# The delta-rule inverse built for all heads at once on 32x32 diagonal blocks, with the scan and the first head norms placed among the gated units

## The reference, cut to what matters

```python
kk = where(strict, k @ k.T * ratio, 0)        # ratio = exp(gc_i - gc_j), causal
a_mat = eye + beta[:, None] * kk
u_v = triangular_solve(a_mat, beta * v)       # unit lower triangular
w_k = triangular_solve(a_mat, beta * gamma * k)
# scan over the chunks, state s:
u = u_v - w_k @ s
o = (q * gamma) @ s + (q @ k.T * ratio) @ u
s = decay * s + (k * exp(gc_last - gc)).T @ u
```

## Time and profile before

| | |
|---|---|
| median of 3 runs | 2479.71 us |
| span of the profiled execution, which is its own time from first to last instruction | 2478.5 us |
| busy in it: TensorE, VectorE, ScalarE, GpSimd | 97%, 70%, 28%, 6% |
| `mixers`, from the first transpose (208.6 us) to the first product of `mix_out` (399.1 us) | 190.5 us |

### The profile page before, as it was taken

The page is one execution under the profiler, slowest core; times in us unless marked ns, Lnnn a source line. Parts: engine busy times, 40 slices in busy tenths (PEclk is TensorE's granted clock), DMA queues, the critical chain, the costliest instruction groups (busy, mean ns, idle before and its releaser), DMA issues. The chain is left out here.

```text
span 2478.5 us, 34266 instructions
## 1 busy us (share of the span) xinstructions
PE 2395.5 (97%) x13948; PEld 1947.8 (79%) x13948; DVE 1727.4 (70%) x2710; ACT 687.3 (28%) x1264; POOL 141.0 (6%) x127
## 2 busy tenths in 40 slices
PE   8998889999999999999999899999999999999997
PEld 6886878987788888887765588888888888888886
DVE  6665777846788874749788787666666886666653
ACT  2212443012211110423677613222202112222200
POOL 0001001001000012000121010000010001000001
PEclk9999989999999999999999999999999999999999
DMA  5220002421233264322200072333463552232341
GB/s 186 76 77 1 3 19 94 147 84 60 85 95 101 92 210 143 127 77 78 76 18 1 35 268 72 100 96 95 163 237 101 186 190 66 94 102 94 127 141 64
DMA packets 70332, 252.81 MB, mean 102 GB/s; under 512 B 7808, under 2 KB 8096, under 8 KB 69664
## 3 DMA queue, kind: packets, MB, share of 16 engines
q1 hardware_dynamic: 69888, 250.08, 30.5%
q10 hardware_dynamic: 288, 0.54, 0.1%
HBM read 248.50 MB, written 2.10 MB: 101 GB/s over the span
## 5 line engine op out<-in xcount | busy, mean ns | idle before, releaser
L393 PE MATMUL psum<-rounded_n,rounded_high 128*128 128x512 f32 x1856 | 736.2, 397 | 4.4 <-DVE rounded_n_low L547 1.8
L395 PE MATMUL psum<-rounded_n,rounded_ring 128*128 128x512 f32 x1856 | 723.9, 390 | 0.0
L394 PE MATMUL psum<-rounded_n_low,rounded_high 128*128 128x512 f32 x1856 | 723.8, 390 | 0.0
L347 DVE TENSOR_TENSOR rounded_ring<-ring,rounded_high 128x1024 fp32r<-128x1024 f32 (+1 forms) x360 | 445.8, 1239 | 38.7 <-ACT rounded_high L330 26.7
L393 PEld LDWEIGHTS psum<-rounded_n,rounded_high 128*128 128x128 f32 x1856 | 349.4, 188 | 85.2 <-issue 7.3
L394 PEld LDWEIGHTS psum<-rounded_n_low,rounded_high 128*128 128x128 f32 x1856 | 349.4, 188 | 76.5 <-issue 5.5
L395 PEld LDWEIGHTS psum<-rounded_n,rounded_ring 128*128 128x128 f32 x1856 | 349.2, 188 | 73.3
L345 DVE CAST rounded_high<-ring 128x1024 fp32r<-128x1024 f32 (+1 forms) x347 | 248.5, 716 | 190.1 <-PE psum L395 183.0
L393 PE MATMUL psum<-rounded_arena,rounded_high 128*128 128x512 f32 x720 | 281.2, 391 | 4.4 <-DVE rounded_ring L347 4.4
L394 PE MATMUL psum<-rounded_arena,rounded_high 128*128 128x512 f32 x720 | 281.0, 390 | 0.0
L395 PE MATMUL psum<-rounded_arena,rounded_ring 128*128 128x512 f32 x720 | 281.0, 390 | 0.0
(11 more groups left out here) (479 smaller groups left out, 2899.4 us busy)
## 6 DMA issues: line engine op xcount, KB each, us to landing
ring<-in_w_up SPq DMA_DIRECT2D x132, 512.0 KB, 3.4
ring<-in_w_down SPq DMA_DIRECT2D x48, 512.0 KB, 3.5
n_low<-in_mod_w SPq DMA_DIRECT2D x48, 512.0 KB, 5.2
arena<-in_mod_w SPq DMA_DIRECT2D x48, 512.0 KB, 5.2
ring<-in_w_ab_in SPq DMA_DIRECT2D x37, 512.0 KB, 3.5
ring<-in_w_mix_in SPq DMA_DIRECT2D x31, 512.0 KB, 3.4
ring<-in_w_sc_in SPq DMA_DIRECT2D x24, 512.0 KB, 5.3
ring<-in_w_down SPq DMA_DIRECT2D x24, 384.0 KB, 3.1
```

What stands on the lines that cost most here:

```text
L347: nc.vector.tensor_tensor(self.rounded(raw), raw, self.rounded(high), ALU.subtract).then_inc(self.weights_split, 1)
L393: self.nc.tensor.matmul(out, w_high, x_high, start=first, stop=False)
L394: self.nc.tensor.matmul(out, w_high, x_low, start=False, stop=False)
L395: return self.nc.tensor.matmul(out, w_low, x_high, start=False, stop=last)
```

## The change

It touches the projection in a few places and rewrites the order of `mixers`.

- **Projection.** `masks` and its DMA go. `mask` multiplies `ratio` by beta as well (4 instructions of 128x128 per head for one of 128x512), `key_tail` multiplies `tail` by beta, and ScalarE copies the 32x32 diagonal blocks of `ratio` into `ratio_c` (`ratio_blocks`, 4 copies). `beta_scale` and the beta in `scan_solved` go. The tiles CK and CQ change places.
- **The inverse.** For levels 1 to 16 only the 16 diagonal 32x32 blocks of each head matter; those of all 4 heads and chunks fit one 128x512 tile. `key_pieces` makes them directly, `first_inverse` does level 0, and four levels follow for all heads at once: 64 products of 32x32x32, a mask, 64 products, a subtraction, and a 32x32-block transpose on VectorE. Two joins give the 64x64 and the 128x128 blocks: two rounds of products each, with copies by ScalarE, and six placing copies on GpSimd. So 24 steps become 4, with the retention between them.
- **The units.** `decayed_pair` makes the halves of queries and keys that a level uses in one 128x512 instruction with an interleaved access pattern, for two. The units 1 and 2 alternate between two pairs of banks (`room`), and their small uses wait for the `take` before the last.
- **The order.** The scan begins at the fifth use, and the first head norms, gates and weight splits stand among units 1 and 2. The filler products of the scan go; 12 stay at the end. The inverse's results are kept in other buffers.

The diff, cut to its core:

```diff
@@ mixer_projection
-            sp.dma_start(k.masks[:], k.dram["masks"]).then_inc(late_landed, 16)
+            def ratio_blocks():
+                act.wait_ge(masked, HEADS)
+                for i in range(4):
+                    rows = slice(32 * i, 32 * i + 32)
+                    nc.scalar.copy(k.ratio_c[rows, :]..., k.ratio[rows, :, :]...[:, :, :, rows])
@@ mask
-                nc.vector.tensor_tensor(r, r, tri, ALU.mult).then_inc(masked, 1)
+                for c in range(TT):
+                    i, r = c * HEADS + h, k.ratio[:, h, c * P:(c + 1) * P]
+                    last = nc.vector.scalar_tensor_tensor(r, r, k.beta[:, i:i + 1], k.const("upto"),
+                                                          ALU.mult, ALU.mult)
@@ mixers, TensorE
+        def piecewise(out, keys, values):
+            for h in range(HEADS):
+                for c in range(TT):
+                    for i in range(4):
+                        last = nc.tensor.matmul(out[rows32(i), piece(h, c)], keys[rows32(i), piece(h, c)],
+                                                values[rows32(i), piece(h, c)], start=True, stop=True)
+        def inverse_times(n):
+            pe.wait_ge(inverse, n)
+            piecewise(k.psum[:, D0, :], k.an, k.xt).then_inc(crossed, 1)
+        def inverse_update(n):
+            pe.wait_ge(mixed_up, n)
+            piecewise(k.psum[:, D0 + 1, :], k.xn, k.pt).then_inc(copied, 1)
-        for x in range(D_STEPS):
-            if x + 1 < D_STEPS:
-                below(HEADS + x + 1)
-            update(HEADS + x)
-            use(x)
+        key_pieces()
+        key_halves()
+        turn(0)
+        inverse_times(1)
+        query_products(0)
+        inverse_update(1)
+        turn(1)
+        query_products(1)
+        inverse_times(2)
...
+        ret_values(7)
+        join_second()
+        use(0)
+        join_third()
+        use(1)
+        join_fourth()
+        use(2)
+        use(3)
+        scan_solve(0)
+        use(4)
+        scan_out(0)
+        use(5)
+        scan_keys(1)
...
+        scan_out(3)
+        use(13)
+        use(14)
+        for i in range(4):
+            norm_sums(pe, i)
+        use(15)
+        use(16)
+        for i in range(3):
+            norm_spread(pe, i)
...
+        pe.wait_ge(valued, 4)
+        for _ in range(8):
+            nc.tensor.matmul(k.psum[:, D0 + 1, 3 * P:T], k.const("ident"), k.const("ones"), start=True, stop=True)
+        for i in (6, 7):
+            norm_sums(pe, i)
@@ mixers, VectorE
+        def first_inverse():
+            dve.wait_ge(paired, 1)
+            link(nc.vector.tensor_tensor(fours(k.ntc, P), pairs_of(D0, 0, P), fours(k.ratio_c, P), ALU.mult))
+            nc.vector.transpose(k.an, k.ntc).then_inc(begun, 1)
...
+            nc.vector.transpose(k.xn, k.xt).then_inc(inverse, 1)
+        def cross_part_of(n):
+            dve.wait_ge(crossed, n)
+            nc.vector.tensor_tensor(quarter(k.pt), quarter(k.psum[:, D0, :]), <mask n>, ALU.mult
+                                    ).then_inc(mixed_up, 1)
+        def update(n):
+            dve.wait_ge(copied, n)
+            link(nc.vector.tensor_tensor(k.xt, k.xt, k.psum[:, D0 + 1, :], ALU.subtract))
+            nc.vector.transpose(k.xn, k.xt).then_inc(inverse, 1)
+        def decayed_pair(t):
+            both = bass.AP(tensor=keys.tensor, offset=keys.offset,
+                           ap=[keys.ap[0], [step + b, 2], [2 * b, T // (2 * b)], [1, b]])
+            nc.vector.tensor_tensor(qk[t % 2]..., both, e[t % 2]..., ALU.mult).then_inc(qk_ready, 1)
-            if FIRST_PICKS + x < HEADS * len(LEVELS):
-                pick(FIRST_PICKS + x)
@@ mixers, GpSimd: six of these for the picks
+            nc.gpsimd.tensor_copy(dst[rows32(i), :, at:at + 32], quarter(src[rows32(i), :])).then_inc(quarters, 1)
```

More of the change, by code:

```diff
@@ L1574, in ret_scores, with query_products @@
+        def query_products(m):
+            pe.wait_ge(weighted, 2 + m)
+            for c in range(TT):
+                cols = slice(c * P, (c + 1) * P)
+                for s in range(2):
+                    rows = head_rows(s)
+                    last = nc.tensor.matmul(k.psum[:, D0 + 2 + s, cols], z[rows, BK + m, cols],
+                                            z[rows, BQ + m, cols], start=True, stop=True)
+            last.then_inc(paired, 1)
         def ret_scores(i):
@@ new lines, in join_second @@
+        def join_second():
+            pe.wait_ge(joints_kept, 1)
+            for h in range(HEADS):
+                for c in range(TT):
+                    at = piece(h, c)
+                    nc.tensor.matmul(k.psum[rows32(1), D0 + 1, at], k.xt[rows32(1), at], k.q32[rows32(1), at],
+                                     start=True, stop=True)
+                    for b in range(2):
+                        rows = rows32(2 * b + 1)
+                        last = nc.tensor.matmul(k.psum[rows32(2 * b), D0 + 1, at], k.q32[rows, at], k.xt[rows, at],
+                                                start=True, stop=True)
+            last.then_inc(joined, 1)
@@ new lines, in join_third @@
+        def join_third():
+            pe.wait_ge(joints_kept, 2)
+            pe.wait_ge(quarters, 2)
+            pe.wait_ge(ret_weighted, 2 * RETS)
+            for h in range(HEADS):
+                for c in range(TT):
+                    at = HD * ((h % 2) * TT + c)
+                    last = nc.tensor.matmul(k.psum[HD:P, D0 + 2 + h // 2, at:at + HD], k.nt64[0:HD, half(h, c)],
+                                            k.x11[0:HD, h * TT + c, :], start=True, stop=True)
+            last.then_inc(joined, 1)
@@ L1635, in small, with join_fourth @@
+        def join_fourth():
+            pe.wait_ge(joints_kept, 5)
+            pe.wait_ge(quarters, 6)
+            for h in range(HEADS):
+                for c in range(TT):
+                    at = HD * ((h % 2) * TT + c)
+                    last = nc.tensor.matmul(k.psum[0:HD, D0 + h // 2, at:at + HD], k.nt64[HD:P, half(h, c)],
+                                            inv_pieces[HD:P, h * TT + c, HD:P], start=True, stop=True)
+            last.then_inc(joined, 1)
         def small(u, s):
@@ L1775, in tensor @@
-        first_inverse(2)
-        first_inverse(3)
-        below(HEADS)
-        pe.wait_ge(ret_kept, 2)
-        for x in range(D_STEPS):
-            if x + 1 < D_STEPS:
-                below(HEADS + x + 1)
-            update(HEADS + x)
-            use(x)
-        pe.wait_ge(xt_new, HEADS * len(LEVELS))
-        def busy(n, bank=D0 + 3):
-            for _ in range(n):
-                nc.tensor.matmul(k.psum[:, bank, 3 * P:T], k.const("ident"), k.const("ones"), start=True, stop=True)
+        inverse_update(2)
@@ L1817, in tensor @@
+        use(18)
         norm_spread(pe, 3)
-        use(D_STEPS + 4)
+        use(19)
+        use(20)
         for i in (4, 5):
             norm_sums(pe, i)
-        busy(8, D0 + 1)
+        use(21)
+        use(22)
+        for i in (4, 5):
+            norm_spread(pe, i)
+        for x in range(23, len(uses)):
+            use(x)
+        pe.wait_ge(valued, 4)
+        for _ in range(8):
+            nc.tensor.matmul(k.psum[:, D0 + 1, 3 * P:T], k.const("ident"), k.const("ones"), start=True, stop=True)
@@ L1822, in tensor @@
         for i in (6, 7):
             norm_sums(pe, i)
-        busy(4, D0 + 1)
-        for i in (4, 5):
-            norm_spread(pe, i)
+        for _ in range(4):
+            nc.tensor.matmul(k.psum[:, D0 + 1, 3 * P:T], k.const("ident"), k.const("ones"), start=True, stop=True)
     def scalar(act):
@@ L1972, in scalar @@
             square(i)
-        for i in range(4):
+        after_use(17)
+        after_use(18)
+        for i in range(2):
             high_part(i)
-        after_use(D_STEPS + 4)
+        after_use(19)
+        after_use(20)
+        for i in (2, 3):
+            high_part(i)
+        norm_root(1)
+        for x in range(21, 25):
+            after_use(x)
+        for i in (4, 5):
+            high_part(i)
+        for x in range(25, len(uses)):
+            after_use(x)
         act.wait_ge(taken, TURNS + len(uses))
@@ L2260, in vector @@
             gate(i)
+        use(21)
+        low_part(2)
         low_part(3)
+        norm_scale(1)
+        use(22)
+        k.split_until(dve, k.first_tile["mix_out"] + 2)
+        use(23)
+        norm_value(4)
+        norm_value(5)
+        for x in range(24, 26):
+            use(x)
+        for i in (4, 5):
+            low_part(i)
+        for x in range(26, len(uses)):
+            use(x)
         dve.wait_ge(taken, TURNS + len(uses))
```

552 lines of the change are left out of this document (281 added, 271 removed).

## The result

The changed kernel takes 2462.7 us, the kernel before 2481.05 beside it: ratio 0.9929, interval [0.9915, 0.9943], so 18.3 us are gained. Forecast were 37 us: the time lies inside the stated range, but the gain is half. Executions in the chip's slower state are left out of the medians and ratios.

What follows compares the result with a forecast made beforehand. The prediction read waiting chains as the bound of the stage's opening and scan, VectorE of old unit 0. Its parts sum to 140.0 us, plus 10 for clock and 4 for order: 154, so 2443 us, range 2424 to 2467.

Steps and rivals of the forecast that it cites:

- the price of the small products in the opening: Inverse's 32x32x32 products at 10 ns each, 1.31 us per 128 records, within an opening of 37.2 us (was 32.5).
- The rival with 20 ns: Inverse's small products cost 20 ns each, adding 10 us, for a time of 2453 us; chance 0.04.
- Unit 0: First unit of the stage: 36.2 us (was 52.2), levels of 2.65 us as a chain, then a serial tail of 16.8.
- 10 us for the clock in the whole stage: A third of about 30 us of TensorE on the path runs at half clock: 10 us more, bounds 0 and 30.
- Unit 1: Second unit of the stage: 27.7 us (was 43.6), six levels of about 2.7, then merge, copies, cross products and spreads.
- the multiply behind the cross factors: At level 3 of a unit, cross factors take 2.4 us on VectorE, about 1.3 beyond ScalarE's time.
- unit 2 and the end: Last parts of the stage: unit 2 to the end of VALUES 33.8 us (was 53.9), end 5.1 (was 8.3).
- the transposes: VectorE's 32x32-block transposes in the inverse take 0.69 us each, twice that at the upper bound.
- its rival at double cost: The interleaved multiply takes twice 0.69 us, adding 13 us over 21 of them, for 2456 us; chance 0.06.
- order effects: Across the stage, 4 us more for GpSimd's placing copies against VectorE and missed waits between the engines' lists.
- The rival of the low clock: Half clock on most of the path outside small levels: 20 to 30 us more, 2453 to 2467 us; chance 0.20.
- my signs of being wrong: An opening over 45 us, a level over 3.5 us, or a clock at 0.5 from opening to end.

Runs made afterwards that it cites:

- e7_rate: Changed kernel with the 64 products of the key products' diagonal blocks issued 17 times over at the stage's start; 2523.1 us in a single execution.
- e1_fill: Changed kernel with 25 filler products of full rows among unit 0's joins, uses and scan steps, to hold the clock up; 2462.0 us.
- e8_both: Changed kernel with 16 products of 128x128 for the 64 first products of each small inverse level, plus fillers in unit 0; 2467.7 us.
- e13_midfill: Changed kernel with 32 first products of 64x64 per small inverse level, plus 23 fillers of full rows in unit 0; 2456.3 us.
- e11_thin: Changed kernel with unit 0's small products issued for two of its four heads only; 2458.5 us in a single execution.
- e5_pair: Kernel before with only the decayed keys and queries made by one interleaved multiply in place of two; 2468.9 us, ratio 0.9952.
- e3_code: Changed kernel with the products of unit 1's five small levels issued three times over; 2476.3 us in a single execution.
- e15_mid: Changed kernel with 32 first products of 64x64 per small inverse level, without fillers, measured again on one chip; 2459.3 us.

## Why the gain was half of the forecast

**The step that failed** is the price of the small products in the opening: "The inverse's 32x32x32 products are priced from L1649, whose 128 records take 1.31 us, 10 ns each. The other bound is 20 ns". The row is right, but it is a burst: in the old kernel such a group came once in 4.5 us, so its instructions were there when it began. The new opening puts ten groups behind each other, and then a group costs the 3.6 us in which its 256 instructions arrive, 28 ns a matmul record, above my upper bound. The opening's 1,527 matmul records in 47.5 us are twelve pieces: 43 us of arrival for an opening forecast at 37.2. How much of its 10.3 us the clock of 0.87 has beside the supply was not separated. The rival with 20 ns had 0.04; it was the right place with too low a price. The Trainium skill's rule that I set aside ("TensorEngine Tiling (Array Packing)", section Instruction Overhead: about 60 cycles a matmul on Trainium2, from which I estimate 25 ns each and 3.2 us for 128) gives nearly the sustained rate that e7_rate shows, 3.6 us for 128, though the engine there stands still for its instructions and does not work slower; a burst of 1.31 us does not refute it.

**Unit 0**, +14.5: the miss splits at 285.2 us, where `big`'s products (L1734) start: up to there 28.9 us for 19.8 forecast, from there 21.8 for 16.8. (The two forecast parts add up to 36.6, not to the 36.2 of the sum.) The tail's 5 us are the clock, by e1_fill, e8_both and e13_midfill, and its price at full clock was right. Of the other 9, some 4 to 6 at most are the supply, by e11_thin; how the rest divides between the joins at half clock and the order of the lists was not separated. The forecast allowed 10 us for the clock in the whole stage and spread them over the tails, and took the small levels to hide it "by the chain of the other two engines"; but VectorE waited for TensorE there for 15 us.

**Unit 1**, +4.4 (2.8 to 4.7 in other profiles): the clock has a part, for the unit was 1 to 2 us shorter at 0.78 than at 0.62. The waits name one step more: in units 1 and 2 TensorE waits 12.8 us in two goes for L2208, the multiply behind the cross factors, for which I had 1.3 us. Unit 2 has the longer of the two and was still right in sum, so this wait alone does not settle it; no run tried it.

**Right**: unit 2 and the end, the transposes (711 ns for 0.69), the interleaved multiply (686 ns; its rival at double cost is gone), VectorE's 90.0 us for "about 95", a clock of 0.73 and 0.75 in units 1 and 2, and VectorE as the bound of the old unit 0 (e5_pair).

**Luck.** The range holds the time because its slow side was made for another cause. The stage took 28.8 us more than the 140.0 at full clock: 10.3 in the opening, 14.5 in unit 0, 4.4 in unit 1, less 0.4 behind it. The forecast had added 14 of them, for the clock and for order effects. The rival of the low clock, 2453 to 2467, has the time in it, but of its 20 to 30 us the runs show 5 as the clock's for certain, in unit 0's tail. (By its own terms, 140 + 30 + 4, it ends at 174 us of stage and 2463, not at 178 and 2467.) Of my signs of being wrong two came, an opening over 45 and levels over 3.5 us, and both meant what I had said.

**From 21.7 to 18.3 us.** The stage gives back 21.7 us in the profile, the spans differ by 19.2. The 2.5 us between are a balance over stages that the change leaves alone. Behind the stage the changed kernel's lead first grows, to 23.4 us. Then it loses 4.8 us in one place, some 690 us after the stage: from 1066 to 1092 us the granted clock was 0.80, in two stretches at half clock of 3.4 and 6.8 us, and 1.00 for the same work before.

```profile
1066.00:1092.00 26.00, 26.00 (x136) 20.82 (x135) 11.78 (x21) 5.58 (x8) 0.00 (x0) 0.80 0.12 41
```

The same two half-clock stretches stand in the profiles of most other versions, in e5_pair too; they are missing in e3_code, e7_rate and e13_midfill. With them missing, e13_midfill has a span 0.9 us shorter than e15_mid's, though its stage is 2 us longer. What brings them on is open.

## What to carry to other kernels

Price many small instructions by a sustained rate and not by a group that came alone: count the records that a stretch issues and hold them against the instruction queue's packets, as one would with bytes and a DMA. Where that queue is nearly always at work, products twice as large and half as many can shorten the stretch although each group executes more slowly; four times as large lost here. And test the smallest part of a large change by itself: one multiply in place of two brought 12 us in the old kernel, without the new inverse, where the whole change brought 18.

## What the runs showed of the hardware

TensorE's instructions arrive in packets of 16 KB, 256 instructions, at best one in 3.3 to 3.8 us (3.6 on average in e7_rate) when they are used up at once; in e7_rate the clock was at half through those groups, and the pace was that of the changed opening, whose clock was 0.87. With 32 moving columns at full clock, a stationary operand of 128x128 took 3.76 us for 32 matmul records (118 ns each), 64x64 2.06 us for 64 (32 ns), 32x32 1.3 us for 128 (10 ns), where tiles share the engine. And the granted clock stood at 0.50, the lower of the two levels, in 26.3 us of which TensorE was busy for 20.8, with short standstills before and in them; in the old unit 0, busy for 25.2 of 31.4 us, it was 1.00. Fillers of full rows in unit 1 brought it from 0.73 to 0.95.
